# Dividing the second attention after its products, and taking the first mixer's sigmoids from the banks, in a two-block transformer kernel

## The chip, the cores and the metric

One core of a Trainium2 chip runs the whole program. The metric is the device time of one execution in microseconds (us). The core's engines work side by side and wait for one another through semaphores: TensorE (PE in the rows; its weight loads are PEld), VectorE (DVE), ScalarE (ACT), GpSimd (POOL) and SyncE (SP, which issues the loads).

## The reference

512 tokens of width 1024 pass through two blocks. The first has a SwiGLU layer, a mixer with four gated recurrent heads (HGRN2) and four spatial gating groups, cross attention to a memory, and a second SwiGLU layer. The second has self attention with eight query heads over two key and value heads, a pooling mixer beside it, and a SwiGLU layer. The two places that the change touches:

```python
# first block, recurrent heads: forget gate and key from one projection fz
log_f = jnp.log(lb + (1.0 - lb) * jax.nn.sigmoid(fz))
k = (1.0 - lb) * jax.nn.sigmoid(-fz)
...
# second block, attention: head dimension 64
s = jnp.einsum('bqkgd,bskd->bkgqs', qblk, k).astype(jnp.float32) * scale
p = jax.nn.softmax(s, axis=-1)
return jnp.einsum('bkgqs,bskd->bqkgd', p.astype(v.dtype), v)
```

## The kernel before

Activations lie transposed: features on the 128 partitions, the 512 tokens along the free axis, tile k of eight. Every projection runs in blocks of 128 output features. A weight block is split into a high part whi and a low part wlo, activations into ahi and alo, and a block is 24 products of 128x128 by 128x512 (ahi with whi, alo with whi, ahi with wlo; eight each). SyncE loads up to six blocks ahead, ScalarE makes whi (L394), GpSimd makes wlo (L399), for some blocks VectorE. `hi_stream` and `lo_stream` at block j do this for block j+3. Blocks take the PSUM banks 0 to 3 in turn; `bank_free` counts the banks that have been read out.

**First mixer.** The 24 blocks of the input projection "in" run with the mixer's work in between, in an order written by hand: `plan[n]` lists what each engine does at block n. Blocks 0 to 3 are the forget projections. VectorE copies each from its bank to mk (L1787), ScalarE then takes two sigmoids of the copy (L1059 to cum, L1060 in place), VectorE makes the gate from them (three operations, L1694 to L1696), ScalarE takes the logarithm of all four (L1065), VectorE sums each over time (the scan, L1700). GpSimd makes the arguments of the decays from the first scan, ScalarE their exponentials (dec, L1069), VectorE multiplies queries and keys with them (qt L1665, kt L1667), and TensorE makes the level products (L2206), 16 at block 5.

**Second attention.** Eight heads, one after another; the code of every engine runs over h, in one fixed order. In TensorE's turn h: the scores of head h+1 (four query tiles, two products each, L2369 and L2370, with head 1's first pair right after the input projection "in2"), the turning of head h's probabilities ps through the banks 3 and 4 (four key tiles, four transposes each, L2418), and the attended products of head h-1 (L2430: fp32, four key tiles, two instructions each, 64 stationary columns, since a head has 64 features; even heads write partitions 0 to 63 of a bank, odd heads 64 to 127). Each group of four score or turn steps is cut in two halves with half of the attended products behind each. In turns 2 to 5 a product of the pooling mixer (L2453) follows into bank 5; from the second on it waits until VectorE has read the bank (`s_py`, by po, tile name rope, L1989).

VectorE takes the row maxima of the scores (L1903), ScalarE the exponentials with the row sum from its accumulator (L1177), VectorE inverts the sum (L1911) and multiplies ps with it (L1912), and only then may TensorE turn ps. The turned tiles go to psT: the first by VectorE (L1964), three by ScalarE (L1211). After two heads ScalarE casts the finished bank to ahi (L1217) and VectorE makes alo (L1969). The pool tiles are cast and subtracted in the same way (L1227, L1982). Then the output projection "out2" starts, with its tiles in the order `OUT2_TILES`.

## Time and profile before

| | us |
|---|---|
| median of three runs | 1740.92 |
| lowest and highest | 1740.75, 1741.7 |
| time of the profiled execution | 1740.76 |
| its span in the trace | 1738.9 |
| TensorE busy | 1701.5 (98%) |
| VectorE, ScalarE, GpSimd busy | 681.1, 589.5, 710.9 |

Times in the trace count from the start of the span. A busy TensorE product is counted from its start to its modelled end, and the next starts before that end, so the distance from start to start is the price of one. "[idle before <-releaser]" at the end of a timeline row is the time that the engine stood still before it and what ended that.

### The profile page before, as it was taken

What the parts mean: (1) busy time and instruction counts of PE and PEld (TensorE: products, weight loads), DVE (VectorE), ACT (ScalarE), POOL (GpSimd) and SP (SyncE); (2) the same over time, 40 slices, a digit from 0 to 9 for tenths busy, and PEclk for the clock granted to TensorE, in tenths of its full rate; (3) what the DMA queues carried; (4) which work ended last, traced back from release to release, by engine and by line L of the source; (5) the groups of instructions that cost most, each with busy time, mean ns of one, the idle gap of its engine ahead of it and who ended that gap; (6) DMA issues with size and microseconds to landing.
All of it is one profiled execution on the core that took longest, in us unless ns stands there. A gap on an engine that the chain in (4) does not pass through costs nothing.

```text
span 1738.9 us, 21093 instructions
## 1 busy us (share of the span) xinstructions
PE 1701.5 (98%) x8525; PEld 1417.6 (82%) x8525; DVE 681.1 (39%) x1122; ACT 589.5 (34%) x890; POOL 710.9 (41%) x386
## 2 busy tenths in 40 slices
PE   7999999998999999999999999999899999999998
PEld 6888888897888789879888888898657988888886
DVE  3111211268776776356211121266884522112122
ACT  4222222256444554236222222246453422222210
POOL 3443444445554343114453444433331454444442
PEclk9999999999999999999999999999999999999999
DMA  6333243333222345212433233342111333323322
GB/s 189 97 97 97 79 116 97 97 110 85 61 61 61 97 125 142 73 49 71 112 97 97 82 112 97 86 128 61 37 37 49 85 98 97 97 82 112 97 85 73
DMA packets 302826, 157.66 MB, mean 91 GB/s; under 512 B 5145, under 2 KB 301194, under 8 KB 302730
## 3 DMA queue, kind: packets, MB, share of 16 engines
q1 hardware_dynamic: 302730, 156.32, 31.6%
q8 instruction: 68, 1.11, 0.3%
q14 instruction: 28, 0.23, 0.1%
HBM read 154.20 MB, written 2.10 MB: 90 GB/s over the span
## 4 chain that ended last, share of the span: by engine, by line
PE 66%; DVE 4%; ACT 3%; issue 2%; POOL 0%; DVEq 0%; ACTq 0%; POOLq 0%
PE bank L434 16%; PE bank L435 16%; PE bank L438 15%; PE bank L2430 1%; PE bank L2054 1%; PE bank L2051 1%; PE bank L2050 1%; PE bank L481 1%; PE bank L482 1%; PE bank L486 1%; PE bank L2206 1%; PE bank L467 1%; PE bank L461 1%; PE bank L462 1%; PE bank L2311 1%
## 5 line engine op out<-in xcount | busy, mean ns | idle before, releaser
L399 POOL TENSOR_TENSOR wlo<-wraw,whi 128x1024 fp32r<-128x1024 f32 (+1 forms) x256 | 608.6, 2390 | 909.9 <-ACT whi L394 909.9
L434 PE MATMUL bank<-ahi,whi 128*128 128x512 f32 x1312 | 516.0, 393 | 0.0
L435 PE MATMUL bank<-alo,whi 128*128 128x512 f32 x1312 | 511.7, 390 | 0.0
L394 ACT CAST whi<-wraw 128x1024 fp32r<-128x1024 f32 (+1 forms) x286 | 285.9, 1025 | 255.4 <-PE bank L438 169.4
L438 PE MATMUL bank<-ahi,wlo 128*128 128x512 f32 x1312 | 324.0, 389 | 0.0
L434 PEld LDWEIGHTS bank<-ahi,whi 128*128 128x128 f32 x1312 | 247.2, 188 | 52.1 <-issue 1.2
L435 PEld LDWEIGHTS bank<-alo,whi 128*128 128x128 f32 x1312 | 247.0, 188 | 52.0 <-issue 1.2
L438 PEld LDWEIGHTS bank<-ahi,wlo 128*128 128x128 f32 x1312 | 246.3, 188 | 51.1
L1377 DVE SCALAR_TENSOR_TENSOR hval<-gate,bank 128x512 f32<-128x512 f32 x66 | 45.4, 688 | 557.2 <-PE bank L438 543.2
L859 ACT ACTIVATE gate<-bank 128x512 f32<-128x512 f32 x66 | 39.6, 600 | 514.9 <-PE bank L438 506.1
L1386 DVE SCALAR_TENSOR_TENSOR res<-res,bank 128x512 f32<-128x512 f32 x80 | 54.1, 686 | 261.7 <-PE bank L438 181.7
L434 PE MATMUL bank<-hid,whi 128*128 128x512 f32 x332 | 130.5, 393 | 0.0
L435 PE MATMUL bank<-hid,whi 128*128 128x512 f32 x332 | 129.9, 391 | 0.0
L438 PE MATMUL bank<-hid,wlo 128*128 128x512 f32 x332 | 83.4, 391 | 0.0
L438 PEld LDWEIGHTS bank<-hid,wlo 128*128 128x128 f32 x332 | 62.3, 188 | 13.7
L434 PEld LDWEIGHTS bank<-hid,whi 128*128 128x128 f32 x332 | 62.4, 188 | 13.4
L435 PEld LDWEIGHTS bank<-hid,whi 128*128 128x128 f32 x332 | 62.4, 188 | 13.4
L1368 DVE TENSOR_TENSOR hid<-hval,hid 128x512 fp32r<-128x512 f32 x66 | 67.2, 1019 | 2.3
L876 ACT ACTIVATE gate<-res 128x256 f32<-128x256 f32 (+1 forms) x48 | 23.4, 488 | 120.5 <-DVE res L1386 66.7
L2050 PE MATMUL bank<-ahi,whi 128*128 128x256 f32 x256 | 63.3, 285 | 0.0
L2051 PE MATMUL bank<-alo,whi 128*128 128x256 f32 x256 | 62.8, 283 | 0.0
L481 PE MATMUL bank<-hid,whi 128*128 128x512 f32 x132 | 52.0, 394 | 0.0
(304 smaller groups left out, 2241.7 us busy)
## 6 DMA issues: line engine op xcount, KB each, us to landing
wraw<-in_ffn_w_gate SPq DMA_DIRECT2D x44, 512.0 KB, 3.8
wraw<-in_ffn_w_up SPq DMA_DIRECT2D x44, 512.0 KB, 3.8
wraw<-in_w_in SPq DMA_DIRECT2D x34, 512.0 KB, 3.9
wraw<-in_ffn_w_down SPq DMA_DIRECT2D x32, 512.0 KB, 4.0
wraw<-in_w_gate SPq DMA_DIRECT2D x22, 512.0 KB, 3.8
wraw<-in_w_up SPq DMA_DIRECT2D x22, 512.0 KB, 3.8
wraw<-in_w_out SPq DMA_DIRECT2D x16, 512.0 KB, 4.4
wraw<-in_w_down SPq DMA_DIRECT2D x16, 512.0 KB, 4.0
```

The lines of the kernel that those rows point to most:

```text
L394: eng.copy(whi[:, b % 4, 0:n], wraw[:, b % RAW, 0:n]).then_inc(hi_ready, 1)
L399: eng.tensor_tensor(wlo[:, b % RAW, 0:n], wraw[:, b % RAW, 0:n], whi[:, b % 4, 0:n], ALU.subtract).then_inc(LO[b][0], 1)
L434: eng.matmul(o, w, xhi[:, k, :], start=(k == 0), stop=False)
L435: eng.matmul(o, w, xlo[:, k, :], start=False, stop=False)
L438: mm = eng.matmul(o, wlo[:, b % RAW, k * P:(k + 1) * P], xhi[:, k, :], start=False, stop=(k == ph.K - 1))
L481: eng.matmul(o, whi[:, b % 4, k * P:(k + 1) * P], hhi[:, k, :], start=(k == 0), stop=False)
L859: act.activation(gate[:, tile % 2, :], bank_of(ph, j)[:, :], ACT.Silu).then_inc(gate_done, 1)
L1368: dve.tensor_tensor(hlo[:, at, :], hval[:, tile % 2, :], hhi[:, at, :], ALU.subtract).then_inc(hidden_ready, 1)
L1377: dve.scalar_tensor_tensor(out=hval[:, tile % 2, :], in0=gate[:, tile % 2, :], scalar=scale, in1=bank_of(ph, j)[:, :], op0=ALU.mult, op1=A ...
L1386: dve.scalar_tensor_tensor(out=res[:, j, :], in0=res[:, j, :], scalar=scale, in1=bank_of(ph, j)[:, :], op0=ALU.mult, op1=ALU.add).then_inc ...
L2050: pe.matmul(o, w, xhi[:, k, at], start=(k == 0), stop=False)
L2051: pe.matmul(o, w, xlo[:, k, at], start=False, stop=False)
```

## The change

**Second attention.** ps stays undivided; TensorE turns it as soon as the head's exponentials are there. sv gets columns of ones beside each value head, and the attended product takes 128 stationary columns, values and ones, so that one half of its bank holds the attended features and the other the sum, on every partition. Each head has a bank of its own (6 or 7). ScalarE takes Ln of the sums and Exp of the negative (`invert_sums`), VectorE multiplies (`divide`) into ao, and ScalarE and VectorE make ahi and alo from ao. The attended products of a head wait for the division of the head two before it. On VectorE the copy of the turned tile stands ahead of the last maxima; the division, the pool tile's subtraction, po and alo follow behind them, at the end of the turn. On ScalarE the inversion, the cast to ahi and the cast of po stand behind the copies.

**First mixer.** ScalarE takes both sigmoids from the bank and frees it; VectorE's four copies are dropped. The second sigmoid does not wait for the first. The gates and logarithms are spread over the blocks 2 to 5, the first scan comes ahead of the last gate, and the low part of block 6's weights goes from GpSimd to VectorE.

The diff, cut to its core:

```diff
-        sv = take("sv", [P, TT, P])
+        sv = take("sv", [P, TT, 5, HD])
...
-            return DVE if b == 1 or b - phases["in"].base in (4, 5) or (b % 2 and blocks[b][0].name in DVE_SPLITS) else POOL
+            return DVE if b == 1 or b - phases["in"].base in (4, 5, 6) or (b % 2 and blocks[b][0].name in DVE_SPLITS) else POOL
...
-        for h in range(HG):
-            plan[1 + h] += [("forget", h)]
-        plan[4] += [("logs", 0)]
+        plan[1] += [("forget", 0)]
+        plan[2] += [("forget", 1)]
+        plan[3] += [("forget", 2)]
+        plan[4] += [("forget", 3), ("log", 0), ("log", 1), ("log", 2)]
+        plan[5] += [("log", 3)]
...
-        OUT2_TILES = [0, 7, 1, 6, 5, 2, 4, 3]
+        def rows_of(h):
+
+            return slice(HD * (h % 2), HD * (h % 2) + HD), slice(HD * (1 - h % 2), HD * (1 - h % 2) + HD)
+
+        OUT2_TILES = [0, 7, 6, 1, 5, 4, 2, 3]
...
-                    wait_in(act, FZ0 + n)
-                    link(act.activation(cum[:, n, :], mk[:, n, :], ACT.Sigmoid))
-                    act.activation(mk[:, n, :], mk[:, n, :], ACT.Sigmoid, scale=-1.0).then_inc(s_sig, 1)
...
+                    at = bank_of(phases["in"], n)[:, :]
+                    wait_block(act, phases["in"], n)
+                    act.activation(cum[:, n, :], at, ACT.Sigmoid)
+                    act.activation(mk[:, n, :], at, ACT.Sigmoid, scale=-1.0).then_inc(bank_free, 1)
...
-                if 1 <= n <= 4:
+                if 1 <= n <= 2:
                     hi_stream(phases["in"], n)
...
-                act.activation(ps[:, h % 2, t, :], score_bank(n)[:, :], ACT.Exp, bias=small[:, c:c + 1],
-                               accum_out=small[:, S_SM + n % 8:S_SM + n % 8 + 1]).then_inc(s_pe, 1)
+                act.activation(ps[:, h % 2, t, :], score_bank(n)[:, :], ACT.Exp, bias=small[:, c:c + 1]).then_inc(s_pe, 1)
...
+            def invert_sums(h):
+
+                own, other = rows_of(h)
+                act.wait_ge(s_pv, 2 * XH + h + 1)
+                if h >= 2:
+                    act.wait_ge(s_pn, TT * XH + h - 1)
+                link(act.activation(rinv[other, h % 2, :], bank[6 + h % 2][other, :], ACT.Ln))
+                act.activation(rinv[own, h % 2, :], rinv[other, h % 2, :], ACT.Exp, scale=-1.0).then_inc(s_si, 1)
+
             def attended_hi(h):
-
                 if h % 2:
-                    act.wait_ge(s_pv, 2 * XH + h + 1)
-                    act.copy(ahi[:, h // 2, :], bank[6 + (h // 2) % 2][:, :]).then_inc(s_ah, 1)
+                    act.wait_ge(s_pn, TT * XH + h + 1)
+                    act.copy(ahi[:, h // 2, :], ao[:, (h // 2) % 2, :]).then_inc(s_ah, 1)
...
-            GATES = {3: (("forget", 0),), 4: (("forget", 1), ("forget", 2), ("forget", 3), ("scan", 0))}
+            GATES = {2: (("forget", 0),), 3: (("forget", 1),), 4: (("forget", 2), ("scan", 0), ("forget", 3))}
...
-                wait_block(dve, phases["in"], n)
-                dve.tensor_copy(IN_DST[n], bank_of(phases["in"], n)[:, :]).then_inc(bank_free, 1)
+                if n >= 4:
+                    wait_block(dve, phases["in"], n)
+                    dve.tensor_copy(IN_DST[n], bank_of(phases["in"], n)[:, :]).then_inc(bank_free, 1)
...
-                link(dve.reciprocal(small[:, S_RI + c:S_RI + c + 1], small[:, S_SM + c:S_SM + c + 1]))
-                dve.tensor_scalar(ps[:, h % 2, t, :], ps[:, h % 2, t, :], small[:, S_RI + c:S_RI + c + 1], None, ALU.mult).then_inc(s_pn, 1)
...
+                    link(dve.memset(sv[:, :, 0:5:2, :], 1.0))
...
+            def divide(h):
+                own, other = rows_of(h)
+                dve.wait_ge(s_si, h + 1)
+                dve.tensor_tensor(ao[own, (h // 2) % 2, :], bank[6 + h % 2][own, :], rinv[own, h % 2, :], ALU.mult).then_inc(s_pn, 1)
+
...
             for h in range(QH):
-                self_normalise(h, TT - 1)
                 self_max(h + 1, 0)
                 self_max(h + 1, 1)
+                take_transposed(h, 0)
+                self_max(h + 1, 2)
+                self_max(h + 1, 3)
                 if h >= 2:
-                    attended_lo(h - 2)
+                    divide(h - 2)
...
-                take_transposed(h, 0)
-                self_max(h + 1, 2)
-                self_normalise(h + 1, 0)
-                self_normalise(h + 1, 1)
-                self_max(h + 1, 3)
-                self_normalise(h + 1, 2)
+                if h >= 2:
+                    attended_lo(h - 2)
+            divide(QH - 2)
+            divide(QH - 1)
             attended_lo(QH - 1)
...
                 if st == 0:
-                    pe.wait_ge(s_pn, TT * XH + TT * (h + 1))
+                    pe.wait_ge(s_pe, TT * XH + TT * (h + 1))
...
-                    if h >= 4 and h % 2 == 0:
-                        pe.wait_ge(*operand("out2", OUT2_TILES.index(h // 2 - 2)))
-                i = pe.matmul(bank[6 + (h // 2) % 2][p0:p0 + HD, :], sv[:, st, HD * (h // 4):HD * (h // 4) + HD],
-                              psT[:, h % 2, st, :], start=(st == 0), stop=(st == TT - 1))
+                    if h >= 2:
+                        pe.wait_ge(s_pn, TT * XH + h - 1)
+                n = 2 * (h // 4) + (h + 1) % 2
+                i = pe.matmul(bank[6 + h % 2][:, :], sv[:, st, n:n + 2, :], psT[:, h % 2, st, :], start=(st == 0), stop=(st == TT - 1))
```

How this stands in a row on two engines at three places. In the changed kernel the line numbers are higher; names are those of the program with their buffer numbers, and what an instruction waits for is in brackets.

VectorE in the second attention, turn h = 3 (the first with po; pool_out is what po signals, pool_products what TensorE's pool product signals). Before:

```order
L1903 TENSOR_REDUCE small_60<-bank1 128x1 [waits scores]
L1903 TENSOR_REDUCE small_60<-bank2 128x1 [waits scores]
L1969 TENSOR_TENSOR alo_52<-bank6,ahi_50 128x512 [waits attended_hi]
L1989 TENSOR_SCALAR rope_117<-bank5,vecs_58 128x512 [waits pool_products]
L1964 COPY psT_116<-bank3 128x512 [waits attended,probabilities_transposed]
L1903 TENSOR_REDUCE small_60<-bank0 128x1 [waits scores]
L1911 RECIPROCAL small_60<-small_60 128x1 [waits probabilities]
L1912 TENSOR_SCALAR ps_115<-ps_115,small_60 128x512 [waits dve_chain]
L1911 RECIPROCAL small_60<-small_60 128x1 [waits probabilities]
```

and now:

```order
L1924 TENSOR_REDUCE small_60<-bank1 128x1 [waits scores]
L1924 TENSOR_REDUCE small_60<-bank2 128x1 [waits scores]
L1975 COPY psT_116<-bank3 128x512 [waits attended,probabilities_transposed]
L1924 TENSOR_REDUCE small_60<-bank0 128x1 [waits scores]
L1924 TENSOR_REDUCE small_60<-bank1 128x1 [waits scores]
L1980 TENSOR_TENSOR ao_121<-bank7,rinv_120 64x512 [waits sums_inverted]
L2007 TENSOR_SCALAR rope_117<-bank5,vecs_58 128x512 [waits pool_products]
L1985 TENSOR_TENSOR alo_52<-ao_121,ahi_50 128x512 [waits attended_hi]
```

po (rope) and the attended pair's alo stood right behind the first two maxima, ahead of the copy of the turned tile. They now stand behind all four maxima and the division, which waits for ScalarE's inverted sums.

ScalarE in the same turn. Before:

```order
L1217 CAST ahi_50<-bank6 128x512 [waits attended]
L1177 ACTIVATE ps_115,small_60<-bank1,small_60 128x512 [waits probabilities_transposed,score_maxima]
L1177 ACTIVATE ps_115,small_60<-bank2,small_60 128x512 [waits score_maxima]
L1227 CAST ahi_50<-rope_117 128x512 [waits pool_out]
L1211 COPY psT_116<-bank4 128x512 [waits attended,probabilities_transposed]
L1177 ACTIVATE ps_115,small_60<-bank0,small_60 128x512 [waits score_maxima]
L1177 ACTIVATE ps_115,small_60<-bank1,small_60 128x512 [waits score_maxima]
L1211 COPY psT_116<-bank3 128x512 [waits attended,probabilities_transposed]
L1211 COPY psT_116<-bank4 128x512 [waits attended,probabilities_transposed]
```

and now:

```order
L1187 ACTIVATE ps_115<-bank1,small_60 128x512 [waits probabilities_transposed,score_maxima]
L1187 ACTIVATE ps_115<-bank2,small_60 128x512 [waits score_maxima]
L1220 COPY psT_116<-bank4 128x512 [waits attended,probabilities_transposed]
L1187 ACTIVATE ps_115<-bank0,small_60 128x512 [waits score_maxima]
L1187 ACTIVATE ps_115<-bank1,small_60 128x512 [waits score_maxima]
L1220 COPY psT_116<-bank3 128x512 [waits attended,probabilities_transposed]
L1220 COPY psT_116<-bank4 128x512 [waits attended,probabilities_transposed]
L1228 ACTIVATE rinv_120<-bank7 64x512 [waits attended]
L1229 ACTIVATE rinv_120<-rinv_120 64x512 [waits act_chain]
L1234 CAST ahi_50<-ao_121 128x512 [waits probabilities_normed]
L1250 CAST ahi_50<-rope_117 128x512 [waits pool_out]
```

The cast of po stood between the exponentials; it and the cast to ahi are now at the end, behind the last two copies and the two activations that invert the sums.

ScalarE at the blocks 0 to 5 of the first mixer's input projection. Before:

```order
L1059 ACTIVATE cum_82<-mk_77 128x512 [waits bank_free]
L1060 ACTIVATE mk_77<-mk_77 128x512 [waits act_chain]
L394 CAST whi_55<-wraw_53 128x1024 [waits block_done,raw_ready1]
L1059 ACTIVATE cum_82<-mk_77 128x512 [waits bank_free]
L1060 ACTIVATE mk_77<-mk_77 128x512 [waits act_chain]
L394 CAST whi_55<-wraw_53 128x1024 [waits block_done,raw_ready2]
L1059 ACTIVATE cum_82<-mk_77 128x512 [waits bank_free]
L1060 ACTIVATE mk_77<-mk_77 128x512 [waits act_chain]
L394 CAST whi_55<-wraw_53 128x1024 [waits block_done,raw_ready3]
L1059 ACTIVATE cum_82<-mk_77 128x512 [waits bank_free]
L1060 ACTIVATE mk_77<-mk_77 128x512 [waits act_chain]
L1001 ACT_TABLE_LOAD
```

and now:

```order
L397 CAST whi_55<-wraw_53 128x1024 [waits block_done,raw_ready1]
L1069 ACTIVATE cum_82<-bank1 128x512 [waits block_done]
L1070 ACTIVATE mk_77<-bank1 128x512
L1069 ACTIVATE cum_82<-bank2 128x512 [waits block_done]
L1070 ACTIVATE mk_77<-bank2 128x512
L397 CAST whi_55<-wraw_53 128x1024 [waits block_done,raw_ready2]
L1069 ACTIVATE cum_82<-bank3 128x512 [waits block_done]
L1070 ACTIVATE mk_77<-bank3 128x512
L1010 ACT_TABLE_LOAD
L1075 ACTIVATE cum_82<-cum_82 128x512 [waits forget_ready] x3
L397 CAST whi_55<-wraw_53 128x1024 [waits block_done,raw_ready3]
L1075 ACTIVATE cum_82<-cum_82 128x512 [waits forget_ready]
```

The sigmoids read the banks, two pairs stand together, and a weight cast moves from ahead of the fourth pair to behind the first three logarithms.

## Rows read from the trace of the kernel before

**Rows 1.** The page, first part: busy time, share of span, instructions.
```profile
PE 1701.5 (98%) x8525; PEld 1417.6 (82%) x8525; DVE 681.1 (39%) x1122; ACT 589.5 (34%) x890; POOL 710.9 (41%) x386
```

**Rows 2.** Timeline of TensorE, first mixer: start, length in us, instructions, idle before.
```profile
414.18 1.98 PE L438 MATMUL bank<-ahi,wlo 128*128 128x512 f32 x8
420.27 3.68 PE L2206 MATMUL bank<-qt,kt 128*128 128x64 f32 x16 [4.12 <-DVE kt L1667]
423.71 0.77 PE L434 MATMUL bank<-ahi,whi 128*128 128x512 f32 x1
...
430.87 1.89 PE L2206 MATMUL bank<-qt,kt 128*128 128x64 f32 x16
```

**Rows 3.** Timeline of ScalarE, first mixer.
```profile
400.53 1.28 ACT L1059 ACT_TABLE_LOAD   x1
...
403.96 0.62 ACT L1059 ACTIVATE cum<-mk 128x512 f32<-128x512 f32 x1
...
410.91 1.28 ACT L1001 ACT_TABLE_LOAD   x1
412.21 2.34 ACT L1065 ACTIVATE cum<-cum 128x512 f32<-128x512 f32 x4
```

**Rows 4.** Timeline of VectorE, first mixer.
```profile
412.35 0.54 DVE L1694 TENSOR_SCALAR cum<-cum,small 128x512 f32<-128x512 f32 x1
...
413.80 1.22 DVE L1700 TENSOR_TENSOR_SCAN cum<-restart,cum 128x512 f32<-128x512 f32 x1
...
417.65 2.57 DVE L1667 TENSOR_TENSOR kt<-mk,dec 128x256 f32<-128x256 f32 x1
```

**Rows 5.** Timeline of GpSimd, first mixer.
```profile
417.40 2.53 POOL L399 TENSOR_TENSOR wlo<-wraw,whi 128x1024 fp32r<-128x1024 f32 x1
```

**Rows 6.** Windows: length, busy us (instructions) by engine, PEclk, DMA share, GB/s.
```profile
422.00:424.00 2.00, 2.00 (x11) 2.00 (x11) 2.00 (x3) 0.34 (x2) 2.00 (x3) 0.50 0.00 0
...
1254.00:1256.00 2.00, 2.00 (x7) 1.65 (x7) 1.08 (x3) 1.37 (x5) 1.92 (x2) 0.50 0.00 0
...
1262.00:1264.00 2.00, 2.00 (x12) 1.18 (x11) 2.00 (x5) 1.69 (x5) 1.84 (x3) 1.00 0.32 78
```

**Rows 7.** Timeline of TensorE, start of the second attention.
```profile
1250.63 0.47 PE L2369 MATMUL bank<-khi,sst 128*128 128x512 f32 x1 [0.88 <-DVE su L1956]
...
1252.87 1.77 PE L2418 MATMUL bank<-mats,ps 128*128 128x128 f32 x8 [1.09 <-DVE ps L1912]
...
1261.73 1.09 PE L2418 MATMUL bank<-mats,ps 128*128 128x128 f32 x8 [3.42 <-DVE ps L1912]
...
1262.89 0.40 PE L2370 MATMUL bank<-klo,sst 128*128 128x512 f32 x1
1263.22 1.93 PE L2430 MATMUL bank<-psT,sv 128*64 128x512 f32 x4
...
1265.41 0.39 PE L2370 MATMUL bank<-klo,sst 128*128 128x512 f32 x1
```

**Rows 8.** Timeline of TensorE, input projection of the second block.
```profile
1203.93 1.88 PE L2376 MATMUL bank<-r,mats 128*128 128x512 f32 x4
...
1205.88 0.40 PE L435 MATMUL bank<-alo,whi 128*128 128x512 f32 x1
```

**Rows 9.** Groups by form, 1200 to 1320: busy us, mean ns | idle before.
```profile
L1177 ACT ACTIVATE ps<-bank,small 128x512 f32<-128x512 f32 x32 | 21.9, 688 | 32.4 <-DVE small L1903 32.1
L1903 DVE TENSOR_REDUCE small<-bank 128x1 f32<-128x512 f32 x32 | 21.2, 682 | 6.0 <-PE bank L2370 5.9
...
L1211 ACT COPY psT<-bank 128x512 f32<-128x512 f32 x24 | 13.2, 585 | 2.3 <-PE bank L2418 2.3
...
L1989 DVE TENSOR_SCALAR rope<-bank,vecs 128x512 f32<-128x512 f32 x4 | 3.2, 803 | 0.0
...
L1969 DVE TENSOR_TENSOR alo<-bank,ahi 128x512 fp32r<-128x512 f32 x4 | 2.7, 686 | 7.2 <-ACT ahi L1217 7.2
```

**Rows 10.** Timeline of TensorE, end of the second attention.
```profile
1314.63 4.51 PE L2430 MATMUL bank<-psT,sv 128*64 128x512 f32 x12
```

More of the change, by code:

```diff
@@ L219, in build @@
         po = rope
+        take = region(WORK + 84 * KB)
+        rinv = take("rinv", [P, 2, T])
+        ao = take("ao", [P, 2, T])
         take = region(0)
@@ L628, in build @@
         s_ah = sem("attended_hi")
+        s_si = sem("sums_inverted")
         s_rope = sem("rope_loaded")
@@ L1057, in mixer @@
                 if kind == "forget":
-                    wait_in(act, FZ0 + n)
-                    link(act.activation(cum[:, n, :], mk[:, n, :], ACT.Sigmoid))
-                    act.activation(mk[:, n, :], mk[:, n, :], ACT.Sigmoid, scale=-1.0).then_inc(s_sig, 1)
-                elif kind == "logs":
-                    use_logs()
-                    for h in range(HG):
-                        act.wait_ge(s_fg, h + 1)
-                        act.activation(cum[:, h, :], cum[:, h, :], ACT.Ln).then_inc(s_lf, 1)
+                    at = bank_of(phases["in"], n)[:, :]
+                    wait_block(act, phases["in"], n)
+                    act.activation(cum[:, n, :], at, ACT.Sigmoid)
+                    act.activation(mk[:, n, :], at, ACT.Sigmoid, scale=-1.0).then_inc(bank_free, 1)
+                elif kind == "log":
+                    if n == 0:
+                        use_logs()
+                    act.wait_ge(s_fg, n + 1)
+                    act.activation(cum[:, n, :], cum[:, n, :], ACT.Ln).then_inc(s_lf, 1)
                 elif kind == "level" and n in NTH:
@@ L1102, in _ @@
                     mixer(*task)
-                if n > 4:
+                if n > 2:
                     hi_stream(phases["in"], n)
@@ L1232, in _ @@
                 take_transposed(h, 3)
+                if h >= 2:
+                    invert_sums(h - 2)
+                    attended_hi(h - 2)
+                if 0 <= h - POOL_AT - 1 < 4:
+                    n = h - POOL_AT - 1
+                    act.wait_ge(s_py, n + 1)
+                    act.copy(ahi[:, 4 + POOL_ORDER[n], :], po[:, n % 2, :]).then_inc(s_pyh, 1)
+            invert_sums(QH - 2)
+            invert_sums(QH - 1)
             attended_hi(QH - 1)
@@ L1779, in _ @@
                 for task in tasks:
-                    if task[0] not in ("forget", "logs"):
+                    if task[0] not in ("forget", "log"):
                         mixer(*task)
@@ L1935, in prepare @@
                     dve.wait_ge(s_svT, 1)
-                    dve.tensor_copy(sv[:, :, :], bank[7][:, :].rearrange("p (n f) -> p n f", f=P)).then_inc(s_dupc, 1)
+                    dve.tensor_copy(sv[:, :, 1:5:2, :], bank[7][:, :].rearrange("p (n g f) -> p n g f", g=2, f=HD)).then_inc(s_dupc, 1)
                 elif kind == "take_k":
@@ L1968, in attended_lo @@
                     dve.wait_ge(s_ah, 2 * XH + h // 2 + 1)
-                    dve.tensor_tensor(alo[:, h // 2, :], bank[6 + (h // 2) % 2][:, :], ahi[:, h // 2, :],
+                    dve.tensor_tensor(alo[:, h // 2, :], ao[:, (h // 2) % 2, :], ahi[:, h // 2, :],
                                       ALU.subtract).then_inc(act_dve, 1)
             for h in range(QH):
-                self_normalise(h, TT - 1)
                 self_max(h + 1, 0)
                 self_max(h + 1, 1)
+                take_transposed(h, 0)
+                self_max(h + 1, 2)
+                self_max(h + 1, 3)
                 if h >= 2:
-                    attended_lo(h - 2)
+                    divide(h - 2)
                 if 0 <= h - POOL_AT - 2 < 4:
@@ L2421, in self_attend @@
             def self_attend(h, st):
-                p0 = HD * (h % 2)
                 if h < 0:
```

18 lines of the change are left out of this document (2 added, 16 removed).

## The prediction

> **What bounds the kernel now.** I read the page first: TensorE is busy for 1701.5 of 1738.9 us [rows 1], so a change pays only where it shortens TensorE's own work or one of its pauses. Next the pauses, in TensorE's timeline. Two places that the change touches have them. In the first mixer TensorE ends a block at 414.18 + 1.98 = 416.16 and starts the level products only at 420.27, after 4.12 us [rows 2]. In the second attention it pauses for 0.88 us, 1.09 us and 3.42 us before the first attended product at 1263.22 [rows 7]; after that it runs almost without pause to 1314.63 + 4.51 = 1319.14 [rows 10]. Last the granted clock: after the 4.12 us pause and after the pair of 0.88 and 1.09 it is 0.50 (1.2 GHz), after the 3.42 us pause it stays 1.00 (2.4 GHz) [rows 6]. So a pause costs itself, and sometimes a stretch at the lower clock behind it.
>
> I make the sum against the profiled execution (1740.76 us, 0.16 under the median of the three runs). Hand-over from engine to engine is 0.05 us: kt ends at 420.22 [rows 4], TensorE starts at 420.27 [rows 2].
>
> **First mixer.** ScalarE's table load ends at 401.81 and the second sigmoid pair starts at 403.96, so a pair and a weight cast take 2.15 [rows 3]. Now ScalarE runs pair, cast, pair, pair, cast, pair without waiting for VectorE's copies: four pairs of about 1.1 (the second sigmoid no longer waits for the first) and two casts of 0.95 bring it to about 408. With the log table (1.30 to the first log [rows 3]) and the first log (0.6) the first scan can start at 409.9 instead of 413.80; VectorE, with a gate set at 1.45 (412.35 to 413.80 [rows 4]), has two of the three sets ahead of it done by then and the third just ending. Behind the scan everything was late by VectorE's kt, 2.57 us instead of 0.4, because it ended only after GpSimd's weight subtraction (417.40 + 2.53 = 419.93 [rows 5]). That subtraction follows the scan too and moves to about 413.5 to 416.0. I let it hold up both qt and kt, so kt is ready at 417.0. TensorE's pause shrinks from 4.12 to 0.9: **3.2 us**. The copies that are dropped (4 x 0.68) and the weight split that VectorE gets instead (1.2) lie beside this. If nothing blocked qt, 0.7 more would come.
>
> The clock there: the 16 level products take 3.44 (420.27 to 423.71), against 1.73 at full clock (1.89 less the 0.16 by which a busy time runs over [rows 2]); of the difference 1.1 is clock and 0.6 the wait for the second kt, which stays. The next block takes 7.16 (423.71 to 430.87) where 24 products at 0.2275 (eight in 1.98 - 0.16 [rows 2]) make 5.46: 1.7. Together 2.8, so at full clock this stage gives 6.0. But 0.9 us of pause with sparse products behind is most like the 0.88 and 1.09 of [rows 7], and those were followed by a low stretch; I charge one, 1.8 us. **Gain 4.2**, bounds 2.5 and 6.7. VectorE and GpSimd behind it move earlier with the scan and have slack of over half a microsecond at each level product; if they had none the lower end holds.
>
> ScalarE: Activation LUTs in the Trainium skill (What ACT_TABLE_LOAD costs) puts a change of set at 2.66 us, of which 1.38 are a drain. [rows 3] show 1.30 from the load to the next activation. By the page the first scan would start 1.4 later and the gain would be 1.4 less; the row decides.
>
> **Second attention, its start.** The scores of head 1 still wait for the last block's copy (1250.63 [rows 7]). Turning head 0 needs only the exponentials now, finished long before, so the 1.09 pause goes. Then ScalarE is the chain: from 1252.1 four exponentials at 0.60 (0.69 less 0.09 of overlap), three copies at 0.49 (0.58 less 0.09) [rows 9] and 0.15 of waiting bring it to 1256.2; half a turn of two (0.44) and one score (0.47) later the first attended product starts at 1257.1, not at 1263.22. **Gain 6.1** with the clock at full; a low stretch would take 1.7, so 4.4 to 6.1. The ones written into sv (1.0 us on VectorE at most, by a 0.68 us operation of 512 columns [rows 9] taken for 768) come before the last blocks of the input projection, which cover them; uncovered they would cost that.
>
> **Attended products of full width.** Those of 64 columns cost more than their own time. From the first of four to the second product of the next score it is 1265.41 - 1263.22 = 2.19; the same number of full-width fp32 products and one more takes 1205.88 - 1203.93 = 1.95 [rows 7, 8]. Going in, 1262.89 to 1263.22 is 0.33 against about 0.235. So 0.34 per group; there are 14 groups: **4.8 saved** (bounds 0 and 4.8). At the end, though, the last twelve are busy for 4.51 [rows 10] where twelve at 0.43 and the run-over of 0.16 make 5.3: head 6 uses the lower half of the columns, head 7 the upper, and two of their products ran at once. Full width loses that: **0.8**. The Trainium skill, TensorEngine Tiling (Array Packing), Key Properties, says both, that a change of tiling mode drains the engine and that tiles work in parallel; by the second alone the change would cost and never save.
>
> **The new wait.** This is the term that decides. TensorE's pool product n ends head n+2, and from n = 1 waits for VectorE's po(n-1) to be done with bank 5. Before, VectorE wrote po early in the same head, ahead of its copy of the turned tile. Now po stands behind the division, the division behind ScalarE's Ln and Exp, and those behind the head's last exponential and last two copies. Count from D, the end of the last score product of a head. VectorE: maximum 0.05 + 0.68. ScalarE: 0.04, exponential 0.60, two copies 0.98, Ln and Exp 0.72 + 0.63 (two activations like those of L1177). VectorE: 0.04, division 0.61, po 0.80 [rows 9]. With the hand-over po is free at D + 5.2. TensorE needs 0.87 for two turns (1.09 with start and run-over [rows 7]) and 1.72 for four attended products, less 0.16, and stands at D + 2.4. **It waits 2.75 us in head 3**, and 3.35 in heads 4 and 5, where the subtraction of the pool tile (0.60) comes ahead of po. What is queued behind is all of the next head's scores. In head 7, where no scores cover it, attended products wait for divisions: 1.2 for head 4's, 0.3 for two copies queued behind it, 1.1 for head 5's. Sum: 2.75 + 6.7 + 2.6 = **12.0 lost**. The divisions of heads 6 and 7 fall under the output projection, whose tile 3 comes last, nearly 10 us in; nothing is charged. The dropped normalisations on VectorE (32 times) and accumulator reads are worth nothing more, since TensorE, not VectorE, set the pace of a head.
>
> The pauses of 2.75 and 3.35 may lower the clock. One of 3.42 did not, one of 4.12 did, two short ones together did [rows 6, 7]. I take two of three at 1.6: **3.2 lost**, bounds 0 and 5.1. TensorE: Matmul & The Clock Gate in the Trainium skill (The HAM clock gate) says the point of a transition varies from run to run, which would put the number of falls anywhere from none to three.
>
> **Sum.** Attention: -6.1 - 4.8 + 0.8 + 12.0 + 3.2 = +5.1. Mixer: -4.2. Together +0.9 or 1.0; from 1740.92 that is 1741.9 us.
>
> **Rivals.**
> (a) The clock never falls after the new waits, and not in the mixer: 3.2 + 1.8 less, 1736.9. For it speaks the 3.42 us pause, against it the others.
> (b) Slower: the clock falls after all three waits and at the start of the attention: +1.9 + 1.7, 1745.5. It needs a third fall in the pool heads; with two and none at the start it stays at the forecast.
> (c) The mixer's gain is given back, because VectorE or GpSimd become what the level products wait for: +4.2, 1746.1. Against it: both start 3.2 earlier themselves.
> (d) The extra time round 64-column products has another cause (the change of operands, say) and stays: +4.8, 1746.7. Against it: full-width fp32 products meet fp32r ones with none [rows 8].
> (e) The po wait is not met, because the chain is shorter than I add up or po is free earlier: -12.0 - 3.2, 1726.7, what the change would give without the new order. I see no way round the wait in the code.
>
> **How the numbers follow.** A measurement of this kernel can tell about 0.2%, 3.5 us. Forecast 50% (its own range 1738 to 1744.5), (a) 16%, (b) 14%, (c) 9%, (d) 7%, (e) 4%. Faster by over 0.2% are (a) and (e): 20%. Slower are (b), (c), (d): 30%. The rest, 50%, is no change. The range from 1736.5 to 1747 takes in all but (e), and what lies beyond the ends of (a) and (d).
>
> **What would show it.** In the profile of the changed kernel: TensorE pausing under 1.5 us before the first level products; no pause over 1 us between head 1's scores and the first attended product; attended products 0.43 apart with no extra step round them; three pauses of 2.7 to 3.4 us in front of pool products 1 to 3, ended by VectorE's po; clock at 0.50 behind one to three of them. Pauses at the pool products under 1 us would sink the forecast downwards; a gap over 3 us in the mixer, upwards.

## The result, and the profile after

The changed kernel takes 1743.62 us in the median of 22 runs, the kernel before 1740.88 in 22 runs beside them: a ratio of 1.0013 with a 95% interval of 1.0007 to 1.0018. That is 2.7 us slower, inside the 0.2% that I had called no change, and 1.7 above the predicted 1741.9. Nineteen of the 22 times lie between 1742.7 and 1744.4, three at 1740.1 to 1740.5 with a higher mean clock (0.997 against 0.993 to 0.996); so the clock doesn't fall equally often in each run.

The profiled execution took 1743.5 us (span 1741.7), 2.7 more than that of before. TensorE is busy for about as long as before (2.9 less) [rows 1]:

```profile
PE 1698.6 (98%) x8525; PEld 1421.5 (82%) x8525; DVE 659.8 (38%) x1064; ACT 595.6 (34%) x874; POOL 708.3 (41%) x385
```

**First mixer.** TensorE's timeline (start, length, instructions, idle before in brackets), beside [rows 2]. All of this execution is 0.79 us later from the start on (414.97 for 414.18, the same block), so differences count from there.

```profile
414.97 1.98 PE L441 MATMUL bank<-ahi,wlo 128*128 128x512 f32 x8
418.26 1.10 PE L2222 MATMUL bank<-qt,kt 128*128 128x64 f32 x8 [1.31 <-DVE kt L1687]
419.80 1.10 PE L2222 MATMUL bank<-qt,kt 128*128 128x64 f32 x8 [0.43 <-DVE kt L1687]
...
426.27 1.89 PE L2222 MATMUL bank<-qt,kt 128*128 128x64 f32 x16
...
442.59 1.10 PE L2222 MATMUL bank<-qt,kt 128*128 128x64 f32 x8 [0.98 <-DVE kt L1687]
```

The pause of 4.12 is 1.31, and the next level products come 5.4 earlier (430.87 - 426.27 + 0.79). But at 442.59 there is a pause of 0.98 that the kernel before did not have. VectorE and then GpSimd, beside [rows 4, 5]:

```profile
410.57 1.22 DVE L1720 TENSOR_TENSOR_SCAN cum<-restart,cum 128x512 f32<-128x512 f32 x1
...
415.03 2.42 DVE L1685 TENSOR_TENSOR qt<-mq,dec 128x256 f32<-128x256 f32 x1 [0.68 <-DVE mq L1808]
417.38 0.83 DVE L1687 TENSOR_TENSOR kt<-mk,dec 128x256 f32<-128x256 f32 x1
```
```profile
414.78 2.39 POOL L402 TENSOR_TENSOR wlo<-wraw,whi 128x1024 fp32r<-128x1024 f32 x1
```

The scan starts at 410.57 (409.9 + 0.79 was forecast), and now it is qt that takes 2.42 beside GpSimd's subtraction. That subtraction comes 0.5 later than the 413.5 + 0.79 forecast: the first three of GpSimd's four operations ahead of it took 0.83, 0.80 and 0.79 beside VectorE's last gate and the copy behind it, where 0.62, 0.62 and 0.61 stood before.

**Second attention.** TensorE's timeline, beside [rows 7, 10]:

```profile
1245.68 0.47 PE L2385 MATMUL bank<-khi,sst 128*128 128x512 f32 x1 [0.88 <-DVE su L1967]
...
1252.22 1.88 PE L2446 MATMUL bank<-psT,sv 128*128 128x512 f32 x4
...
1264.03 1.02 PE L2468 MATMUL bank<-su,poolw 128*128 128x512 f32 x2
...
1270.20 1.88 PE L2446 MATMUL bank<-psT,sv 128*128 128x512 f32 x4
```
```profile
1274.76 2.05 PE L2468 MATMUL bank<-su,poolw 128*128 128x512 f32 x2 [2.67 <-DVE rope L2007]
...
1282.59 1.88 PE L2446 MATMUL bank<-psT,sv 128*128 128x512 f32 x4
1287.75 1.51 PE L2468 MATMUL bank<-su,poolw 128*128 128x512 f32 x2 [3.28 <-DVE rope L2007]
...
1295.63 1.88 PE L2446 MATMUL bank<-psT,sv 128*128 128x512 f32 x4
1300.90 1.10 PE L2468 MATMUL bank<-su,poolw 128*128 128x512 f32 x2 [3.39 <-DVE rope L2007]
...
1308.77 1.88 PE L2446 MATMUL bank<-psT,sv 128*128 128x512 f32 x4
...
1312.61 1.96 PE L2446 MATMUL bank<-psT,sv 128*128 128x512 f32 x4 [1.08 <-DVE ao L1980]
...
1318.40 3.67 PE L2446 MATMUL bank<-psT,sv 128*128 128x512 f32 x8 [0.92 <-DVE ao L1980]
1321.51 0.80 PE L464 MATMUL bank<-ahi,whi 128*128 128x512 f32 x1
```

From the first score of head 1 to the first attended product it is 6.54 (1252.22 - 1245.68), before 12.59 [rows 7]. Then come three pauses at the pool products, and in head 7 two for divisions. The windows (length, busy time by engine, granted clock third from the end) show the clock there, beside [rows 6]:

```profile
422.00:424.00 2.00, 2.00 (x10) 1.65 (x9) 1.87 (x4) 0.00 (x0) 2.00 (x2) 1.00 0.00 0
1275.00:1277.00 2.00, 2.00 (x3) 0.90 (x4) 0.20 (x1) 0.26 (x1) 0.00 (x0) 0.50 0.00 0
1289.00:1291.00 2.00, 2.00 (x7) 1.46 (x6) 0.69 (x1) 0.12 (x1) 0.00 (x0) 0.50 0.00 0
1302.00:1304.00 2.00, 2.00 (x8) 1.51 (x7) 1.01 (x2) 0.45 (x1) 0.00 (x0) 0.50 0.00 0
```

It is 1.00 in the mixer, and 0.50 (1.2 GHz) behind all three waits. From a pool product to the second group of attended products of the next head it is 7.83, 7.88 and 7.87 there, against 6.17 (1270.20 - 1264.03) where no wait stood before: each low stretch costs 1.66 to 1.71, together 5.1.

**The balance of the two profiles.** Mixer, from the end of the block ahead of the level products to a pause 139 us later: 139.42 for 145.14, -5.7. Start of the attention -6.05 (6.54 for 12.59). From the first attended product to the first product of the output projection +13.44 (1321.51 - 1252.22 = 69.29, before 1319.07 - 1263.22 = 55.85). The late start of this execution +0.8, and 0.3 behind the attention. Sum +2.8, as the spans say. Between the mixer and the attention nothing changes, although this profile has a low stretch at 1172 to 1176, behind a pause of 2.04 that both kernels have, and that of before has none: from that pause to head 1's first score it is 74.71 (1245.68 - 1170.97) for 74.65 (1250.63 - 1175.98).

### The profile page after: what moved, and what is told of

Same layout as the page of the kernel before. It is cut to its first block, busy times and chain, and to the rows that moved or that the text cites. A ratio compares the mean times of both kernels' runs of the same rounds, so it can differ in the third digit from the quotient of the medians.

```text
span 1741.7 us, 21024 instructions
## 1 busy us (share of the span) xinstructions
PE 1698.6 (98%) x8525; PEld 1421.5 (82%) x8525; DVE 659.8 (38%) x1064; ACT 595.6 (34%) x874; POOL 708.3 (41%) x385
## 4 chain that ended last, share of the span: by engine, by line
PE 86%; DVE 6%; ACT 5%; issue 3%; DMA 0%; POOL 0%; SPq 0%; DVEq 0%; ACTq 0%; POOLq 0%
PE bank L437 21%; PE bank L438 21%; PE bank L441 21%; PE bank L484 2%; PE bank L485 2%; PE bank L489 2%; PE bank L2070 2%; PE bank L2067 2%; PE bank L2066 2%; PE bank L470 1%; PE bank L464 1%; PE bank L465 1%; PE bank L2446 1%; ACT res L908 1%; PE bank L2327 1%
```

## The experiments

All times are medians, with ratios to the kernel before on the same chip.

### 1. The two parts of the change, each alone

The mixer's part alone (sigmoids from the banks, logarithms one by one, the new places of the gates, block 6's split on VectorE), and the attention's part alone. The edit is the diff of the change, cut in two.

> The kernel before with the mixer's part of the change alone; the second attention is as before. Theory: the mixer's gain is real and lasts to the end. In the changed kernel's trace all later pauses stand 4.9 us earlier than before although its first block started 0.8 us later, so this kernel should be 5 to 6 us faster than before: ratio 0.9967, near 1735.3 us, with the pause ahead of the first level products near 1.3 us and no 0.50 clock in the mixer. Rival (c), gain given back later: ratio 0.999 to 1.000, near 1741. Rival (clock falls in the mixer after all, in most runs): ratio 0.9978, near 1737.

> The kernel before with the second attention's part of the change alone; the mixer is as before. Theory: the two parts are independent, so this is the changed kernel (+2.7) less the mixer alone (-3.7): +6.4 over before, near 1747.4 us, ratio 1.0037, made of 6.0 less at the attention's start, 3 to 4 less by full width, 12 of waits and 3.4 to 5 of clock. Rival: the parts interact (the clock falls less often in one of the two), and it is 1744 to 1745.

**Mixer alone: 1737.35 us, ratio 0.9978 (0.9968 to 0.9987).** That is 3.7 faster, less than the 5 to 6 expected and near the 1737 of the second rival, a clock that falls in the mixer after all. Its TensorE timeline and its granted clock:

```profile
417.58 1.10 PE L2209 MATMUL bank<-qt,kt 128*128 128x64 f32 x8 [1.32 <-DVE kt L1669]
...
442.39 1.00 PE L2209 MATMUL bank<-qt,kt 128*128 128x64 f32 x8
```
```profile
421.00:423.00 2.00, 2.00 (x6) 1.56 (x5) 1.87 (x4) 0.19 (x1) 2.00 (x2) 0.50 0.00 0
```

Here the clock did fall behind the 1.32 pause, and yet the level products at 442.39 are only 0.5 later than those of the changed kernel (442.59, less the 0.68 by which that execution runs later), without its pause of 0.98. From the end of the block to the pause near 485 it is 72.13 before, 68.36 here and 67.97 in the changed kernel: 3.8 and 4.2 gained. So at full clock TensorE meets a wait for kt instead, and the low stretch costs 0.4 in this place, not 1.8. Of the six profiled executions with this mixer only the changed kernel's is without the low stretch behind the pause of 1.31 or 1.32 (this one and those of experiments 3, 4 and 5 have it).

The remaining 1.6 of the 5.7 above is a low stretch near 490 that the profiled execution of before has and that of the changed kernel has not. Of the others with the changed mixer three have it (both kernels of experiment 4, and 5) and two have not (this one and 3); with the mixer of before two have it (the attention alone, and the kernel before in experiment 6) and one has not (2). So it is not tied to the change. All eleven profiles have either this stretch, which costs 1.6, or the one near 1172, which costs next to nothing, and never both; what decides between them no run here shows.

**Attention alone: 1746.16 us, ratio 1.0030 (1.0018 to 1.0041).** 5.3 slower, where 6.4 was expected from the difference; with the mixer's -3.7 it makes +1.6 against the +2.7 measured, within the intervals. The same three pauses (2.67, 3.28, 3.39) are there, but in the profiled execution the clock fell behind the first two of them only (the first and the third are shown):

```profile
1281.00:1283.00 2.00, 2.00 (x7) 1.51 (x7) 1.05 (x2) 0.49 (x1) 0.00 (x0) 0.50 0.00 0
...
1306.00:1308.00 2.00, 2.00 (x10) 1.30 (x10) 0.86 (x3) 0.29 (x1) 0.00 (x0) 1.00 0.00 0
```

The same pauses, the same work: two falls here, three there. The number of falls behind like pauses is not fixed.

### 2. Full width in the kernel before

```
-        sv = take("sv", [P, TT, P])
+        sv = take("sv", [P, TT, 5, HD])
...
+                    link(dve.memset(sv[:, :, 0:5:2, :], 0.0))
...
-                i = pe.matmul(bank[6 + (h // 2) % 2][p0:p0 + HD, :], sv[:, st, HD * (h // 4):HD * (h // 4) + HD],
-                              psT[:, h % 2, st, :], start=(st == 0), stop=(st == TT - 1))
+                n = 2 * (h // 4) + (h + 1) % 2
+                i = pe.matmul(bank[6 + (h // 2) % 2][:, :], sv[:, st, n:n + 2, :],
+                              psT[:, h % 2, st, :], start=(st == 0 and h % 2 == 0), stop=(st == TT - 1 and h % 2 == 1))
```

> The kernel before, with its second attention's attended products 128 columns wide instead of 64: 64 columns of the weights are zeros, and the two heads of a bank accumulate into it. Nothing else is changed, no order, no wait, no count of products. Theory: the extra time around the 64-column products is the price of going in and out of that shape, 0.34 in each of 14 groups, 4.8, less about 0.5 for the overlap lost in the last twelve products: ratio 0.9975, near 1736.6 us. Rival (d), another cause (new operands, fp32 beside fp32r): it stays, ratio 1.000 to 1.0005, near 1741.4.

**1738.25 us, ratio 0.9985 (0.9976 to 0.9994)**: 2.8 faster. The extra time does belong to the shape, so rival (d) is out. TensorE's timeline, first of the kernel before, then of this one; the rows are the second groups of attended products in the turns 1 and 6 in each, and of this one also the end:

```profile
1266.61 1.93 PE L2430 MATMUL bank<-psT,sv 128*64 128x512 f32 x4
...
1308.63 1.93 PE L2430 MATMUL bank<-psT,sv 128*64 128x512 f32 x4
```
```profile
1265.78 1.88 PE L2431 MATMUL bank<-psT,sv 128*128 128x512 f32 x4
...
1304.64 1.88 PE L2431 MATMUL bank<-psT,sv 128*128 128x512 f32 x4
1307.16 1.09 PE L2419 MATMUL bank<-mats,ps 128*128 128x128 f32 x8 [0.64 <-DVE ps L1912]
...
1310.74 5.32 PE L2431 MATMUL bank<-psT,sv 128*128 128x512 f32 x12
```

Five heads, with ten groups, take 42.02 before and 38.86 here: 3.16, or 0.32 a group. Four of the five heads gain 0.67 to 0.69 (0.34 a group, as forecast), the fourth 0.44, since there TensorE's weight load waits 0.35 for VectorE's copy of turned tile 0: a shorter head leaves VectorE less time. At the end the pause for VectorE's normalisation is 0.64 and was 0.16, and the last twelve products are busy for 5.32 instead of 4.51 [rows 10]: the overlap is lost, 0.8 as the prediction has it and 0.3 more than the 0.5 expected here. Full width is worth less in a kernel whose VectorE still normalises: these two waits are 0.7 of the 1.7 by which the expectation was missed. Another 0.5 is the low stretch at the attention's start, which fell on waiting before and on attended products here. With the 0.3 of overlap 0.2 remain, less than the interval can tell.

### 3. po written ahead of the division again

On VectorE the pool tile's subtraction and po are ahead of the copy of turned tile 0 (their first lines stand for them):

```
                 self_max(h + 1, 1)
+                if 0 <= h - POOL_AT - 2 < 4:
...
+                if 0 <= h - POOL_AT - 1 < 4:
...
                 take_transposed(h, 0)
                 self_max(h + 1, 2)
                 self_max(h + 1, 3)
                 if h >= 2:
                     divide(h - 2)
-                if 0 <= h - POOL_AT - 2 < 4:
...
-                if 0 <= h - POOL_AT - 1 < 4:
```

On ScalarE the cast of po goes from the head's end to behind the second exponential:

```
                 self_exp(h + 1, 1)
+                if 0 <= h - POOL_AT - 1 < 4:
...
                 take_transposed(h, 1)
```

> The changed kernel with two steps put back where they stood before: VectorE writes po (and subtracts the pool tile) ahead of its copy of turned tile 0, and ScalarE casts po after the second exponential. Theory: the pauses before pool products 1 to 3 (2.67, 3.28, 3.39) and the three low-clock stretches behind them (5.1 together) come from po standing behind the division; both go: 9.3 + 5.1 = 14.4 us less than the changed kernel, ratio to before 0.993, near 1729 us; head 7's two waits (2.0) stay. Rival: VectorE's or ScalarE's order makes another wait in each head (the copy of turned tile 0, now behind po, or the inversion), and half or more stays: 1736 to 1742, with new pauses over 1 us in heads 2 to 6.

**1731.89 us, ratio 0.9947 (0.9935 to 0.9960)**: 11.7 less than the changed kernel, 9 less than the kernel before, and 2.9 more than the 1729 expected. What TensorE waits for in the attention (total, times, longest), first in the changed kernel (without head 7's two waits for divisions, 2.0), then here:

```profile
PE bank L2468 <- DVE rope L2007: 9.3, 3, 3.4
```
```profile
PE bank L2446 <- DVE ao L1980: 2.1, 2, 1.2
PE bank L2434 <- DVE psT L1975: 2.0, 2, 1.0
```

The 9.3 are gone and with them all low stretches between 1245 and 1727. But 2.0 come back as waits for the copy of turned tile 0, the rival's kind, in heads 4 and 6. VectorE's timeline shows why:

```profile
1272.77 0.69 DVE L1980 TENSOR_TENSOR ao<-bank,rinv 64x512 f32<-64x512 f32 x1 [2.85 <-ACT rinv L1229]
1274.15 0.69 DVE L1985 TENSOR_TENSOR alo<-ao,ahi 128x512 fp32r<-128x512 f32 x1 [0.69 <-ACT ahi L1234]
1274.87 1.29 DVE L1924 TENSOR_REDUCE small<-bank 128x1 f32<-128x512 f32 x2
...
1276.68 0.81 DVE L2002 TENSOR_SCALAR rope<-bank,vecs 128x512 f32<-128x512 f32 x1
1277.40 0.68 DVE L1975 COPY psT<-bank 128x512 f32<-128x512 f32 x1
```

The late division still stands at the head's end; behind an odd head's come ScalarE's cast and VectorE's subtraction, so VectorE begins the next head at 1274.87 and po and the copy are late. The po wait was moved in part, not only removed: the division still waits 2.85 us for the late inversion. Whether that is the cause, the next experiment tests.

### 4. Inversion and division early, with po early and with po late

On ScalarE, where the call of invert_sums at the head's end is taken out, and on VectorE:

```
             for h in range(QH):
+                if h >= 2:
+                    invert_sums(h - 2)
                 self_exp(h + 1, 0)
```

```
                 take_transposed(h, 0)
+                if h >= 2:
+                    divide(h - 2)
                 self_max(h + 1, 2)
                 self_max(h + 1, 3)
-                if h >= 2:
-                    divide(h - 2)
```

One kernel has this beside the edit of experiment 3. The other has this alone, with po where the change put it.

> As the run with po put back, and in addition ScalarE inverts a head's sums at the start of the second head after it (ahead of the exponentials) and VectorE divides right after its copy of turned tile 0, so that no head's end waits for a division. Theory: the two waits for divisions in head 7 (2.0 us in the changed kernel's trace) go too: 2 us less than the run with po put back, ratio 0.992, near 1727 us. Rival: the inversion ahead of the exponentials (1.35 us) holds up the exponentials and with them the turns, a wait of 0.3 to 0.5 us in each of six heads: near 1730, no better than with po alone.

> The changed kernel with the inversion of a head's sums at the start of ScalarE's part of a head and the division right after VectorE's copy of turned tile 0, while po and its cast stay where the change put them, at the head's end. Theory: what makes po late is not its own place but the chain inversion, division ahead of it. Without the chain VectorE reaches po 0.05 + 0.68 after the last score product and has it 0.8 or 1.4 later, 2.2 at most, before TensorE is there (2.4): no pause at the pool products, none in head 7, as the run with all of it early, near 1727 us, ratio 0.992. Rival: its place at the end is enough for a wait, so that pauses over 1 us at the pool products stay: 1732 or more.

**Both early: 1726.73 us, ratio 0.9917 (0.9904 to 0.9931). Inversion and division early, po late: 1726.14, ratio 0.9915 (0.9902 to 0.9929).** They can't be told apart, and both are 17 us under the changed kernel. What TensorE waits for between 1246 and 1310 is the same in both: one wait of 0.9 for the last copy ahead of head 1's scores, and this one.

```profile
PE bank L2435 <- ACT psT L1220: 0.3, 1, 0.3
```

So po's place is harmless; what stood ahead of it, the inversion and the division, was not. The two were moved together, so their shares are not told apart. In the second, VectorE writes po right behind the head's last maximum, without an idle time ahead of it:

```profile
1271.18 0.81 DVE L2008 TENSOR_SCALAR rope<-bank,vecs 128x512 f32<-128x512 f32 x1
```

The inversion at a head's start (1.35 us on ScalarE) costs TensorE nothing that these rows show. Nothing in the program keeps it at the head's end: turn h inverts the sums of head h-2, and TensorE completes these in turn h-1.

### 5. The waits filled

```
                     if n:
+                        pe.wait_ge(s_pca, XH + 3 * h + 2)
+                        for _ in range((0, 9, 12, 12)[n]):
+                            pe.matmul(bank[3][:, :], sst[:, h, 0:P], khi[:, 0, :], start=True, stop=True)
                         pe.wait_ge(s_py, n)
```

> The changed kernel; while TensorE waits for po ahead of pool products 1, 2 and 3 it does 9, 12 and 12 further products of 128x512 (2.0, 2.7 and 2.7 us at 0.2275) into bank 3, which nothing reads before the next head writes it anew. Order and waits of all other work are as in the changed kernel, and po comes as late. Theory: the three stretches at half clock behind the waits are caused by TensorE standing still in them, so they go while the waits stay: next heads at full clock, 5.1 us less than the changed kernel in its profiled run and 4 to 5 in the median, near 1739 us, ratio to before 0.999. Rival: the clock falls for another reason (the kind of work in a head, say), or the filling takes as much as it saves: 1743.5 or more, ratio 1.0015.

**1738.16 us, ratio 0.9985 (0.9976 to 0.9994)**, 5 less than the changed kernel by the two ratios, with more work on TensorE and po just as late. TensorE's timeline at the first of the three, and the granted clock behind the first and the third (it is 1.00 behind the second too):

```profile
1272.17 2.59 PE L2469 MATMUL bank<-khi,sst 128*128 128x512 f32 x9
1275.27 1.13 PE L2471 MATMUL bank<-su,poolw 128*128 128x512 f32 x2 [0.51 <-DVE rope L2007]
```
```profile
1275.00:1277.00 2.00, 1.73 (x6) 1.11 (x7) 0.92 (x3) 0.65 (x2) 0.00 (x0) 1.00 0.00 0
...
1299.00:1301.00 2.00, 2.00 (x14) 1.72 (x13) 1.28 (x3) 0.55 (x1) 0.00 (x0) 1.00 0.00 0
```

From the first score of head 1 to the output projection it is 70.80 against 75.82: 5.0, the price of the three low stretches and of nothing else. So it is TensorE's standing still that brings them; the price and the wait are separate terms.

### 6. Who does block 7's split in the mixer

On the kernel of experiment 4 with both early, and then on the kernel before (there with 4, 5, 7):

```
-            return DVE if b == 1 or b - phases["in"].base in (4, 5, 6) or (b % 2 and blocks[b][0].name in DVE_SPLITS) else POOL
+            return DVE if b == 1 or b - phases["in"].base in (4, 5, 6, 7) or (b % 2 and blocks[b][0].name in DVE_SPLITS) else POOL
```

> As the run with all of it early (1726.7 us), and in addition the weight split of block 7 of the first mixer's input projection is done by VectorE instead of GpSimd. Theory: TensorE's pause of 1.32 ahead of the first level products is GpSimd's subtraction (413.40 to 415.81 in that run), beside which VectorE's first qt took 2.44 us instead of 0.4; on VectorE the split takes 1.23, of which 0.68 is idle time, so kt is ready some 1.5 earlier and the pause is nearly gone: 1.3 us less, and if the clock does not fall behind it 1.7 more: 1724 to 1725.5. Rival: the level products wait for something else by then, or the split on VectorE holds up qt as long: no gain, 1726.7.

> The kernel before with one number changed: VectorE, not GpSimd, does the weight split of block 7 of the first mixer's input projection. Sigmoids, scan and the order of the gates stay as before. It asks what the mixer's part of the change was worth against the smaller cause of the same wait. Before, the split ran on GpSimd at 417.40 to 419.93 and VectorE's kt took 2.57 beside it. Theory: with the split on VectorE (1.22, in its idle 1.45 ahead of qt) kt is ready near 418.1 instead of 420.2 and TensorE's pause is 2.0 instead of 4.12: 2.1 us less, 1738.8, and if the low clock behind it is shorter, up to 1.7 more, 1737.1, which is what the mixer's whole part gave (1737.35). Rival: the pause is set by the late scan and not by GpSimd, so that kt stays near 420: no gain, 1740.9.

**On the early kernel: 1723.59 us, ratio 0.9901 (0.9887 to 0.9914)**, 3.1 less than without. VectorE's timeline, then TensorE's:

```profile
412.54 1.62 DVE L402 TENSOR_TENSOR wlo<-wraw,whi 128x1024 fp32r<-128x1024 f32 x1
...
414.84 0.86 DVE L1688 TENSOR_TENSOR kt<-mk,dec 128x256 f32<-128x256 f32 x1
```
```profile
415.75 2.19 PE L2223 MATMUL bank<-qt,kt 128*128 128x64 f32 x16 [0.54 <-DVE kt L1688]
```

The pause is 0.54 instead of 1.32, and the granted clock from 418 to 420 is 1.00, where it was 0.50 behind the pause of the kernel without. From the end of the block to the pause near 484 it is 66.8 us for 68.3, 1.6 less. So 1.6 is the split's own worth in the rows. Another 1.6 between the two profiles is the low stretch near 490 that only the other one has; whether the medians differ by 3.1 because this edit keeps it away stays open.

**On the kernel before: 1738.86 us, ratio 0.9988 (0.9979 to 0.9997)**, 2.0 less, as the theory said, but its profile shows less. VectorE, GpSimd and TensorE:

```profile
415.16 1.27 DVE L399 TENSOR_TENSOR wlo<-wraw,whi 128x1024 fp32r<-128x1024 f32 x1
...
418.28 0.83 DVE L1667 TENSOR_TENSOR kt<-mk,dec 128x256 f32<-128x256 f32 x1
```
```profile
415.31 1.60 POOL L1299 TENSOR_TENSOR dec<-cum 128x256 f32<-128x256 f32 x1
```
```profile
419.16 2.18 PE L2206 MATMUL bank<-qt,kt 128*128 128x64 f32 x9 [3.39 <-DVE kt L1667]
```

Now it is GpSimd's second dec operation that is held up beside VectorE's split (1.60 instead of 0.62), so qt, which needs it, comes later, and kt starts at 418.28 instead of 417.65 [rows 4]; only its own 0.83 instead of 2.57 makes it ready 1.1 earlier. The pause is 3.39, not 2.0. From the end of the block to the pause 144 us later the profile gains 0.8 (144.38 for 145.14); the medians say 2.0 with an interval of 0.5 to 3.7. Both profiles have the low stretch near 490. The profiled execution is 0.7 above the median of its kernel, whose times spread over 2.2, so part of the 2.0 may be how often that stretch of 1.6 comes; that is not shown. So one number brings 1 to 2 of the 3.7 that the mixer's whole part brings.

The rest is the earlier scan, but what made it earlier is not taken apart. The change also moved block 6's split to VectorE. In the kernel before it ran on GpSimd from 406.27 to 408.68, and beside it VectorE's timeline has 2.70 for a gate operation that takes 0.48 or 0.49 in the other three gates:

```profile
406.26 2.70 DVE L1696 TENSOR_SCALAR mk<-mk,small 128x512 f32<-128x512 f32 x1
```

The copy of the fourth forget block stood behind it, and ScalarE's fourth sigmoid waited 1.28 for that copy. So a part of the gain may be block 6's split alone, as for block 7; no run here has the split moved and the sigmoids left.

## Why the prediction was right, and which terms were off

- **First mixer, -4.2: right in size, wrong in its parts.** The scan (409.9 + 0.79 forecast, 410.57 found), the blocking by GpSimd's subtraction (kt forecast at 417.0 + 0.79, found at 418.21) and the pause (0.9 forecast, 1.31 found) were as worked out, each 0.4 too early in the forecast. The step "at full clock this stage gives 6.0" failed: it gives 5.4 up to the next level products, for the longer pause and 0.2 behind it, and 4.2 in all, because a wait of 0.98 for kt comes at 442.59. I had written that VectorE and GpSimd "have slack of over half a microsecond at each level product"; at that one they don't. Rival (c) is true for about 1.2 of the 6.0. And the low stretch that I charged at 1.8 costs 0.4, as the same wait hides it. The two errors cancel, which is luck: 3.7 in experiment 1. By the Trainium skill's figure for a change of activation set (ScalarE: Activation LUTs, What ACT_TABLE_LOAD costs) the scan would have come at 411.3 + 0.79; the trace has it 1.5 earlier.
- **Attention's start, -6.1: right.** 6.05 found, and no low stretch.
- **Full width, -4.8 + 0.8: right in this kernel.** Of the +13.44, 12.28 are waits and 5.07 clock; what is left is -3.9, or -3.6 with 0.3 that falls behind the first product of the output projection. 0.34 a group is confirmed by four of five heads in experiment 2.
- **New waits, +12.0: right.** From the end of the work ahead (0.16 less than the busy time says) the three are 2.84, 3.44 and 3.55, for which 2.75, 3.35 and 3.35 stood, and head 7 has 2.45 for 2.6. Sum 12.28. Experiments 3 and 4 show where they come from: not from po's own place but from the inversion and division ahead of it. In the prediction the chain was right; the sentence on rival (e), "I see no way round the wait in the code", was right of the changed kernel only. With inversion and division early the same change is worth -14 to -15 instead of +2.7; the 1726.7 that rival (e) gave as its worth without the new order was met by experiment 4 (1726.73 and 1726.14).
- **Clock at the waits, +3.2: too small.** In the profiled execution the clock fell three times at 1.7, 5.1, the upper bound. This is the step of the term that was mis-sized, and with it rival (b) is half true: three falls behind the waits, none at the attention's start. The attention alone showed two falls behind the same pauses. The Trainium skill says that the point of a transition varies from run to run (TensorE: Matmul & The Clock Gate, The HAM clock gate); these two traces agree, as far as two programs with the same pauses can tell.
- **The sum.** For the profiles: -5.7 (with the stretch near 490 that only before had), -6.1, -3.6, +12.3, +5.1, and +0.8 of a later start give +2.8. The clock at the waits is 1.9 above its term. The other differences (mixer -1.5, of which the stretch near 490 is 1.6, full width +0.4, waits +0.3, late start +0.8) happen to cancel; that the sum then misses by the third fall alone is in part luck.
- **Rivals.** (a) does not fit the median; the three times near 1740.3 are nearest to it. (c) holds in part, (d) is excluded by experiment 2, (e) by the pauses.

The best version measured is that of experiment 6 (change, inversion and division early, block 7's split on VectorE): 1723.59 us, 17 below the kernel before.

## What to carry to other kernels

When a chain of small operations is put ahead of one that frees a buffer, add up the chain against what TensorE has left to do before it needs the buffer: here 5.2 against 2.4 made three waits and turned a gain of 14 us into a loss of 3. Then ask how early the chain itself could start, rather than where the freed operation stands. And price a pause twice, once for itself and once for the clock behind it (1.7 us here where TensorE sets the pace, 0.4 where another engine does).

## What the runs showed of the hardware that I had not expected

- A low stretch costs by what bounds the work in it: 1.66 to 1.71 us in attention heads, 0.4 in the mixer, where TensorE would have waited for VectorE's kt at full clock (67.97 against 68.36 us for the same work), and under 0.1 near 1172, ahead of the second attention (74.71 against 74.65).
- The same three pauses of 2.67, 3.28 and 3.39 us brought three falls in one program and two in another; pauses of 1.31 and 1.32 in the mixer brought a fall in each of five executions and none in a sixth, the changed kernel's. Filled with products, down to about half a microsecond, they brought none.
- VectorE and GpSimd hold each other up in both directions: qt took 2.42 us beside GpSimd's subtraction, and a 0.62 us operation of GpSimd took 1.60 beside VectorE's.
- Four fp32 products of 64 columns between products of 128 cost 0.34 us more than four of 128, in the eight groups of experiment 2 beside which no wait changed.
